# A two-block transformer kernel on one core: 150 TensorE products into an unread bank, beside the query and key norms of the first two layers

## The reference, cut to what matters

```python
def rms_norm(x, g):
    xf = x.astype(jnp.float32)
    y = xf * lax.rsqrt(jnp.mean(xf * xf, axis=-1, keepdims=True) + EPS)
    return (y * g.astype(jnp.float32)).astype(x.dtype)
...
def even_layer(x, mem_n, pos, layer, norm_g, w_in, ...):
    h = rms_norm(x, norm_g)
    a_u, a_v, a_g, b_q, b_k, b_v, b_g, m_q, m_g = split_cols(h @ w_in, EVEN_SPLITS)
    y_a = chunked_sgu(jax.nn.gelu(a_u), jax.nn.gelu(a_v), a_ws, a_bs, a_vnorm) * jax.nn.silu(a_g)
    ...
    q = rms_norm(b_q.reshape(Bz, S, B_HEADS, 2, B_QK_DIM), b_qnorm).transpose(0, 2, 3, 1, 4)
    k = rms_norm(b_k.reshape(Bz, S, B_HEADS, 2, B_QK_DIM), b_knorm).transpose(0, 2, 3, 1, 4)
    q, k = rope_partial(q, pos), rope_partial(k, pos)
    ...
```

## Time and profile before

| what | us |
|---|---|
| median of 3 runs | 3789.98 (3786.57 to 3794.05) |
| the profiled execution | 3787.69 |
| its span, first to last instruction | 3785.8 |
| TensorE busy (matmul) | 3046.0 (80% of the span) |
| VectorE busy | 1307.3 (35%) |
| ScalarE busy | 609.0 (16%) |
| mean granted TensorE clock | 0.898 of full speed |

### The profile page before, as it was taken

The page is one execution under the profiler, slowest core; times in us unless marked ns, Lnnn a source line. Parts: engine busy times, 40 slices in busy tenths (PEclk is TensorE's granted clock), DMA queues, the critical chain, the costliest instruction groups (busy, mean ns, idle before and its releaser), DMA issues. The chain is left out here.

```text
span 3785.8 us, 44643 instructions
## 1 busy us (share of the span) xinstructions
PE 3046.0 (80%) x18941; PEld 1819.4 (48%) x18941; DVE 1307.3 (35%) x2504; ACT 609.0 (16%) x1273; POOL 240.5 (6%) x344
## 2 busy tenths in 40 slices
PE   4993986998497679988999972739879849888888
PEld 2441753445276345557888841326434334333333
DVE  1006531007854159615556524374101231111111
ACT  1002321001242135312112101113110010000000
POOL 0000100000010000003333300000000000000000
PEclk9996698997688889998999986869999969999999
DMA  3120003126200311000000021200121039999998
GB/s 135 67 72 14 1 21 88 56 68 223 108 1 1 120 48 45 32 24 2 3 2 2 2 87 60 89 1 1 45 89 67 33 138 393 413 413 412 412 413 356
DMA packets 161246, 431.74 MB, mean 114 GB/s; under 512 B 33006, under 2 KB 44530, under 8 KB 159893
## 3 DMA queue, kind: packets, MB, share of 16 engines
q1 hardware_dynamic: 161050, 428.90, 30.2%
HBM read 418.22 MB, written 10.66 MB: 113 GB/s over the span
## 5 line engine op out<-in xcount | busy, mean ns | idle before, releaser
L242 PE MATMUL banks<-weight_ring,rows_turned 128*128 128x512 f32 (+1 forms) x1024 | 428.0, 579 | 28.7 <-DMA weight_ring<-in_w_in 23.8
L242 PEld LDWEIGHTS banks<-weight_ring,rows_turned 128*128 128x128 f32 x1024 | 192.4, 195 | 264.5 <-issue 240.5
L242 PE MATMUL banks<-weight_ring,branch_turned 128*128 128x512 f32 x640 | 281.3, 601 | 25.2 <-PEq L1119 22.2
L1857 PE MATMUL banks<-rows_turned,weight_ring 128*128 128x256 f32 (+1 forms) x768 | 253.2, 490 | 0.8 <-PEq L379 0.5
L2808 PE MATMUL banks<-expert_weights_early,chosen_turned 128*64 128x512 f32 (+1 forms) x864 | 208.7, 559 | 21.7 <-DMA expert_weights_early<-in_w_up 17.1
L242 PEld LDWEIGHTS banks<-weight_ring,branch_turned 128*128 128x128 f32 x640 | 122.7, 193 | 181.5 <-issue 181.5
L1857 PEld LDWEIGHTS banks<-rows_turned,weight_ring 128*128 128x128 f32 x768 | 147.7, 193 | 99.7 <-issue 84.8
L2808 PE MATMUL banks<-weight_ring,chosen_turned 128*64 128x512 f32 (+1 forms) x672 | 173.3, 570 | 13.1 <-DMA weight_ring<-in_w_up 10.5
L273 DVE COPY projected<-banks 128x512 f32<-128x512 f32 (+1 forms) x28 | 18.4, 655 | 359.6 <-PE banks L242 359.6
L242 PE MATMUL banks<-weight_ring,mix_turned 128*128 128x512 f32 x320 | 138.3, 594 | 2.2 <-PEq L379 1.9
L2808 PEld LDWEIGHTS banks<-expert_weights_early,chosen_turned 128*64 128x64 f32 x864 | 75.4, 137 | 129.9 <-issue 125.9
(11 more groups left out here) (513 smaller groups left out, 4549.5 us busy)
## 6 DMA issues: line engine op xcount, KB each, us to landing
expert_weights_early<-in_w_gate SPq DMA_DIRECT2D x36, 1408.0 KB, 19.4
expert_weights_early<-in_w_up SPq DMA_DIRECT2D x36, 1408.0 KB, 16.8
expert_weights_early<-in_w_down SPq DMA_DIRECT2D x44, 1024.0 KB, 18.7
weight_ring<-in_w_gate SPq DMA_DIRECT2D x28, 1408.0 KB, 19.7
weight_ring<-in_w_up SPq DMA_DIRECT2D x28, 1408.0 KB, 17.8
weight_ring<-in_w_down SPq DMA_DIRECT2D x36, 1024.0 KB, 17.7
weight_ring<-in_l_w_in SPq DMA_DIRECT2D x15, 2048.0 KB, 8.5
weight_ring<-in_w_in SPq DMA_DIRECT2D x13, 2048.0 KB, 7.8
```

The source lines that it names most:

```text
L242: ins = nc.tensor.matmul(kit.ps[0:m, u % 8, 0:cols], lhsT, rhs, start=(k0 + j == 0), stop=(k0 + j == matrix.nk - 1))
L1857: ins = nc.tensor.matmul(kit.ps[:, bank(u), 0:n], w[:, k, f * P:(f + 1) * P], hT[:, k, h0:h0 + n], start=(k == 0), stop=(k == KD - 1))
```

## The change

A new helper issues `count` products of the 128x128 identity with 128x512 values, all into bank 7, with no semaphore before or behind them. It is called with 80 as TensorE's program in the first layer's `elementwise` stage, which had none, and with 70 at the end of TensorE's program in the second layer's. Nothing reads bank 7 before a later stage has written it anew. The values that it streams (`BV` of token tile 0, and columns 1024 to 1535 of `tb`) are not written in these stages.

```diff
+def keep_awake(kit, pe, rows, count):
+
+    for _ in range(count):
+        kit.nc.tensor.matmul(kit.ps[:, 7, :], kit.ident, rows, start=True, stop=True)
...
-            elementwise(kit, vector=vector, scalar=scalar)
+            elementwise(kit, vector=vector, scalar=scalar, tensor=lambda pe: keep_awake(kit, pe, y[:, 0, BV:BV + 512], 80))
...
                 turn_sums(len(ada_groups) - 1)
+                keep_awake(kit, pe, tb[:, 0, KV:KV + 512], 70)
```

## The result

The changed kernel takes 3816.82 us (median of 4 runs, 3809.48 to 3820.33) against 3788.28 for the kernel before: the ratio is 1.0071, with a 95% interval from 1.0051 to 1.0092. It is slower, by 28.5 us on the medians; the forecast was 34.7. The profiled execution took 3814.68, which is 27.0 over that of before.

A forecast was written before the change was run, and what follows sets the result against it. Both norms stages were taken as bound by VectorE and ScalarE, with TensorE idle, until the products outlast them. 17.1 - 2.1 + 22.6 - 2.9 = +34.7 us gave 3824.7 us, range 3812 to 3834.

The forecast's parts named there:

- A product costs 0.866 us: Each added product is two records of 0.433 us at 2.4 GHz, so 0.866 us.
- The rival of products at half the price: Added products take one record each, fit behind the norms, and the time is 3785 us; chance 4 in 100.
- The first stage, +17.1: First layer's norms stage: 80 products outlast VectorE and ScalarE, so transposes start at 375.1 instead of 357.96, +17.1 us.
- Its transposes, -2.1: First layer's transposes start at the high clock, so their 4.36 us at the low clock shrink to about half, -2.1 us.
- The second stage, +22.6: Second layer's norms stage: 70 products move the transposes' start from 1015.02 to 1037.7, cold start included, +22.6 us.
- I had taken 2.6 us: Second layer's products start at the low clock; loss until it rises put at 2.6 us, bounds 0 and 3.0.
- Its transposes, -2.9: Second layer's transposes regain half of the 6.08 us at the low clock, -2.9 us, bounds 0 and -3.0.
- a few microseconds either way: Allowance in the forecast's range for low-clock stretches behind the two changed places moving; three earlier runs differ by 7.5 us.
- the attention's low stretch would be as before: First layer's attention, about 62 us at clock 0.50: same low stretch, later by the shift, costed at nothing.
- the pause ahead of it fells the clock: TensorE's idle time from 371.0 to the first layer's attention lowers the clock there, and the change leaves it.
- My figure for it, -26.4: First layer's attention at full clock: 61.9 us become 35.5; part of the rival that the clock stays up, 3 in 100.
- The last rival: Transposes do not hold the clock, so it falls within them: about +11 us on top, 3836 us; chance 3 in 100.

The follow-up runs named there:

- double_first: The changed kernel with 160 products in the first layer instead of 80, 70 in the second as before; 3880.13 us in one run.
- bridge: The changed kernel with 60 and 43 products instead of 80 and 70, to shorten the pause before the transposes; 3777.37 us, ratio 0.9987 to the kernel before.
- second_only: The changed kernel without the first layer's call: 70 products in the second layer only; 3803.58 us, ratio 1.0042 to the kernel before.
- held: `bridge` plus four products in the small stage before the first layer's attention and one 256-column, full-height product in 18 attention steps; 3759.76 us, ratio 0.9959.
- tail: `fit` plus four products in the pause of the small stage before the first layer's attention; 3781.42 us, ratio 0.9999 to the kernel before.
- thin: `fit` with products that use 32 rows of the array instead of 128; 3871.91 us in one run.
- fillers_only: `held` without the 60 and 43 products beside the norms of the two layers; 3760.33 us, ratio 0.9940 to the kernel before.
- with_transposes: The changed kernel with 440 and 320 transposes of 128x128 in place of its products; 3783.55 us in one run.
- held_less: `held` with attention fillers of 128 columns instead of 256; 3773.44 us, ratio 0.9976 to the kernel before.
- fit: The changed kernel with 58 and 42 products instead of 80 and 70, to end before the last Silu; 3782.44 us, ratio 0.9992 to the kernel before.

## Why the prediction was right

The direction, the mechanism and the four terms hold.

- **A product costs 0.866 us.** 68.90 us for 80 products is 0.861, and `double_first` gives 0.858 for each of the second 80, a little under the 0.866. The rival of products at half the price is out: the records are 160.
- **The first stage, +17.1.** The transposes start 16.8 us later (374.76 against 357.96). With 60 products (`bridge`) the transposes start at 357.00; `double_first` shows that what comes behind the stage's end stands in the open to the last product.
- **Its transposes, -2.1.** At the small stage's products the lag is 14.7 (382.00 against 367.31), so -2.1.
- **The second stage, +22.6.** TensorE's last gate row starts 12.45 us later than before (985.33 against 972.88), the transposes 34.4 later: +22.0. The difference is mostly the cold start. I had taken 2.6 us, and it cost 1.8, with the clock back 3.4 us behind the first product (987.12 to 990.5). This is no fixed term: in `second_only` the same products behind the same gate rows had the clock only 5.9 us on (972.36 to 978.26) and took 63.27 us, which is 3.1 for the cold start.
- **Its transposes, -2.9.** The lag at the compressed scores is 31.5 (1057.62 against 1026.16, where the scores' first record stood before), so -2.9.

These terms sum to 33.8 in the profiled run, against 34.7 foretold. The remaining 6.8 us, down to the 27.0 of the whole span, went elsewhere, in places that the change does not touch: 2.2 between the first layer's spatial products and the last gate row of the second, 1.3 to the second layer's output, 2.5 to the second block's keys, and the rest behind. I had given the low stretches behind the places "a few microseconds either way", and they came out on one side. The traces show that it went with these stretches, whose time I added up from rows of 1 us. The attention's was 61.4 us long before (375.98 to 437.42) and 58.0 after (389.76 to 447.80), and the way from the first layer's spatial products to its output products is 1.4 us shorter. Between the second layer's output and the second block's keys it was 201 us before and 195 after.

From the second layer's transposes to its output products the program is the same in every kernel here. In the fourteen traces this way took 197 to 218 us, and each of these times is half of what it spent at the low clock plus 166 to 171 us: 197.5 in `bridge` with 57 us at the low clock, 200.2 with 61 in the changed kernel, 204.5 with 71 before, 210.2 with 82 in `held`. So one kernel's low stretches can be 13 us dearer than another's where nothing was changed. What sets their length, no run here shows. Each kernel has one trace, so it is open too whether another execution of the changed kernel has them like this (its four runs lie 10.9 us apart).

The prediction said that the attention's low stretch would be as before, and it was. But the reason I gave, that the pause ahead of it fells the clock, was wrong. `tail` filled the pause and the clock fell all the same. So that this part came true was luck as far as its reason goes. `thin` shows that TensorE at work on 32 rows alone is let down, and `fillers_only` that full-height products in the attention keep the clock up; whether they do it by their height or by their amount is open. The same mistaken reason made me set the value of the attention's low stretch aside as out of reach. My figure for it, -26.4, was of the right size: `fillers_only` got 20.9 of it, after paying for its 18 products.

The last rival, that transposes do not hold the clock, is out by `with_transposes`.

## What to carry to other kernels

Before filling an idle engine to keep its clock, count what the low clock costs: only the time in which that engine has work at the low level, here 4.4 and 6.1 us, halved, and not the 100 us that the clock row shows. Count the filling work against the stage it hides in: past that end every product is paid in full, and one that ends microseconds early lost the clock again. A stretch at the low clock in which TensorE is busy is where to look: here 18 short products of full height between small ones, with four before them, gave 23 us, where 103 products beside the norms gave 5, in an interval that nearly reaches nothing. And a gain or loss of a few microseconds should be read off the traces at the place itself: the low stretches of the rest moved by more than that.

## What the runs showed of the hardware that I had not expected

- A TensorE that is busy without a gap with products of 32 rows fell to 1.2 GHz within 2.4 us (304.9 to 307.3) and stayed there for 95 us: 0.84 us a record against 0.43 for 128 rows of the same 512 columns. The Trainium skill (page "TensorE: Matmul & The Clock Gate", section "Why this matters for your kernels") states that a single product of 32 rows takes the same time as one of 128. That holds here only at an equal clock.
- One product of 128 rows and 256 columns in 18 of the first 19 steps kept the clock at 2.4 GHz through an attention in which it had been at 1.2 for 62 us; one of 128 columns left it at 1.2 GHz from 375.4 to 413.0 (`held_less`).
- A pause of 2.66 us between products and transposes was followed by the fall of the clock (`fit`), one of 0.94 us was not (`bridge`). It can go either way at nearly the same length: in the second layer of `with_transposes` the pause was 2.72 us, and the first 24 transposes behind it took 2.81, which is the full clock's pace.
- Transposes alone held the full clock for 48 us.
